# Expert activations taken in pairs on ScalarE, in the PEER stage of a two-block transformer kernel

## The reference

```python
def block(args):
    xc, ic, gc = args                       # 128 tokens, their expert numbers and gates
    u = jnp.take(expert_u, ic, axis=0)
    act = jax.nn.gelu(jnp.einsum('cd,ced->ce', xc, u).astype(jnp.float32), approximate=False)
    vv = jnp.take(expert_v, ic, axis=0)
    return jnp.einsum('ce,ced->cd', (gc * act).astype(vv.dtype), vv)
```

## Time and profile before

| | |
|---|---|
| median of 3 runs | 2718.56 us (2718.0 to 2720.35) |
| profiled execution, its own time | 2720.35 us |
| its span, first to last instruction | 2718.2 us |
| mean granted TensorE clock | 0.958 of full speed |
| busy share of the span: PE, DVE, ACT, POOL | 86%, 58%, 43%, 36% |
| bytes moved by DMA | 771 MB, of these 545 MB by GpSimd's queue |
| first and last gather issued | 657.34 and 1956.95 us |

### The profile page before, as it was taken

The page is one execution under the profiler, slowest core; times in us unless marked ns, Lnnn a source line. Parts: engine busy times, 40 slices in busy tenths (PEclk is TensorE's granted clock), DMA queues, the critical chain, the costliest instruction groups (busy, mean ns, idle before and its releaser), DMA issues. The chain is left out here.

```text
span 2718.2 us, 46334 instructions
## 1 busy us (share of the span) xinstructions
PE 2350.4 (86%) x17098; PEld 1367.4 (50%) x17098; DVE 1578.7 (58%) x3721; ACT 1156.7 (43%) x2887; POOL 990.7 (36%) x687
## 2 busy tenths in 40 slices
PE   7998799988999987777777777877889988889996
PEld 5775699956454532222222222222269777643333
DVE  6786765466566667676767667666454474420003
ACT  4535433344344454444444444444354333433343
POOL 0000211111345366676666766666601000123331
PEclk9999899989999999999999999999999957989998
DMA  8753200063999999999999999999932310389994
GB/s 312 296 198 119 83 4 4 12 253 144 393 416 409 417 411 421 421 421 421 421 419 414 415 417 411 411 421 417 381 111 79 101 32 2 150 328 371 363 365 161
DMA packets 156929, 771.24 MB, mean 284 GB/s; under 512 B 34192, under 2 KB 52256, under 8 KB 71200
## 3 DMA queue, kind: packets, MB, share of 16 engines
q0 software_dynamic: 87552, 545.34, 49.0%
q1 hardware_dynamic: 68144, 220.64, 21.5%
q10 hardware_dynamic: 1008, 2.29, 0.2%
HBM read 816.42 MB, written 16.78 MB: 307 GB/s over the span
## 5 line engine op out<-in xcount | busy, mean ns | idle before, releaser
L2239 PE MATMUL bank<-expert_rows,diagonals 128*128 128x512 f32 x1656 | 802.8, 610 | 176.9 <-ACT diagonals L2131 176.2
L2029 POOL DMA_INDIRECT expert_rows<-in_uv,expert_idx x414 | 629.7, 1521 | 464.3 <-PE bank L2239 297.4
L2064 DVE SCALAR_TENSOR_TENSOR expert_rows<-expert_rows,h_rows 128x1024 f32<-128x1024 f32 x414 | 507.4, 1226 | 328.5 <-DMA expert_rows<-in_uv,expert_idx 327.5
L2239 PEld LDWEIGHTS bank<-expert_rows,diagonals 128*128 128x128 f32 x1656 | 288.6, 189 | 636.9 <-ACT diagonals L2131 412.5
L2123 ACT ACTIVATE expert_act<-expert_dot 128x1 f32<-128x1 f32 x512 | 103.7, 203 | 692.2 <-DVE expert_rows L2064 535.1
L2239 PE MATMUL bank<-weight_slots,diagonals 128*128 128x512 f32 x392 | 193.5, 617 | 47.5 <-ACT diagonals L2131 46.9
L2131 ACT ACTIVATE diagonals<-ident,expert_weight 128x128 f32<-128x128 f32 x512 | 205.4, 401 | 16.7
L2029 POOL DMA_INDIRECT weight_slots<-in_uv,expert_idx x98 | 175.6, 1792 | 67.5 <-issue 50.7
L2064 DVE SCALAR_TENSOR_TENSOR weight_slots<-weight_slots,h_rows 128x1024 f32<-128x1024 f32 x98 | 120.1, 1225 | 88.6 <-DMA weight_slots<-in_uv,expert_idx 83.7
L2127 ACT ACTIVATE expert_weight<-expert_act,expert_gate 128x1 f32<-128x1 f32 x512 | 150.8, 295 | 17.2 <-ACT expert_act L2123 0.2
L2239 PEld LDWEIGHTS bank<-weight_slots,diagonals 128*128 128x128 f32 x392 | 66.6, 189 | 172.2 <-ACT diagonals L2131 119.1
(11 more groups left out here) (566 smaller groups left out, 4025.0 us busy)
## 6 DMA issues: line engine op xcount, KB each, us to landing
expert_w<-in_experts SPq DMA_DIRECT2D x55, 1024.0 KB, 12.1
expert_w_more<-in_experts SPq DMA_DIRECT2D x41, 1024.0 KB, 10.4
mod_rows<-in_ada_rows SPq DMA_DIRECT2D x32, 1024.0 KB, 6.7
weight_slots<-in_w_in SPq DMA_DIRECT2D x8, 1536.0 KB, 7.1
mixed<-in_ada_rows SPq DMA_DIRECT2D x10, 1024.0 KB, 5.0
weight_slots<-in_w_in SPq DMA_DIRECT2D x4, 2048.0 KB, 9.9
weight_slots<-in_att_bias SPq DMA_DIRECT2D x8, 1024.0 KB
weight_slots<-in_w_out SPq DMA_DIRECT2D x4, 2048.0 KB, 8.5
```

The costliest lines, as they stand in the source:

```text
L2029: pool.indirect_dma_start(rows[j], None, core.dram["uv"], bass.IndirectOffsetOnAxis(idx[:, t, column:column + 1], 0)).then_inc(arrived[j], 16)
L2064: dve.scalar_tensor_tensor(out=u, in0=u, scalar=1.0, in1=hN[:, t, :], op0=ALU.mult, op1=ALU.mult, accum_out=dot[:, j:j + 1]).then_inc(dott ...
L2239: mm = pe.matmul(bank[2 * (t % 2) + half][:, :], diag[:, j, :], rows[slot_of(n)][:, D + half * S:D + half * S + S], start=column == 0, sto ...
```

## The change

ScalarE takes the steps in pairs. It waits for two products, makes one gelu of two columns, then two weights, then two diagonals. Each weight still has its own gate, and each diagonal its own matmuls. VectorE's wait for a place in `expert_dot` and the columns at which work between blocks is done are written in terms of pairs. The copies of the query banks come after the pair that follows the one in which a bank was filled.

```diff
-    DEPTH, AHEAD = 8, 2
+    DEPTH, PAIR, AHEAD = 8, 2, 2
...
                     if n >= DEPTH:
-                        dve.wait_ge(gelued, n - DEPTH + 1)
+                        dve.wait_ge(gelued, (n - DEPTH) // PAIR + 1)
...
-                    if t >= 1 and column == 5:
+                    if t >= 1 and column == 3 * PAIR - 1:
                         add_block(t - 1)
-                    if t >= 1 and column == 64:
+                    if t >= 1 and column == 32 * PAIR:
                         invert_block(t - 1)
...
-                for n in range(N):
+                for pair in range(N // PAIR):
+                    n = pair * PAIR
                     (t, column), j = divmod(n, HK), n % DEPTH
                     if n % TOPK == 0:
                         act.wait_ge(topk.head_ready, 2 * (n // TOPK) + 2)
-                    act.wait_ge(dotted, n + 1)
+                    act.wait_ge(dotted, n + PAIR)
                     if n >= DEPTH:
-                        act.wait_ge(weighed, n - DEPTH + 1)
-                    act.activation(act_out[:, j:j + 1], dot[:, j:j + 1], ACT.Gelu).then_inc(gelued, 1)
-                    act.wait_ge(gelued, n + 1)
-                    if n >= DEPTH:
-                        act.wait_ge(diagonal, n - DEPTH + 1)
-                    act.activation(weight[:, j:j + 1], act_out[:, j:j + 1], ACT.Identity, scale=gates[:, t, column:column + 1]).then_inc(weighed, 1)
-                    act.wait_ge(weighed, n + 1)
-                    if n >= DEPTH:
-                        act.wait_ge(slot_free, n - DEPTH + 1)
-                    act.activation(diag[:, j, :], core.ident[:, :], ACT.Identity, scale=weight[:, j:j + 1]).then_inc(diagonal, 1)
+                        act.wait_ge(weighed, n - DEPTH + PAIR)
+                    act.activation(act_out[:, j:j + PAIR], dot[:, j:j + PAIR], ACT.Gelu).then_inc(gelued, 1)
+                    act.wait_ge(gelued, pair + 1)
+                    for i in range(PAIR):
+                        if n >= DEPTH:
+                            act.wait_ge(diagonal, n - DEPTH + i + 1)
+                        act.activation(weight[:, j + i:j + i + 1], act_out[:, j + i:j + i + 1], ACT.Identity,
+                                       scale=gates[:, t, column + i:column + i + 1]).then_inc(weighed, 1)
+                    for i in range(PAIR):
+                        act.wait_ge(weighed, n + i + 1)
+                        if n >= DEPTH:
+                            act.wait_ge(slot_free, n - DEPTH + i + 1)
+                        act.activation(diag[:, j + i, :], core.ident[:, :], ACT.Identity, scale=weight[:, j + i:j + i + 1]).then_inc(diagonal, 1)
                     for u in range(EARLY, len(units)):
-                        if ended[u] + 2 == n:
+                        if ended[u] // PAIR + 1 == pair:
                             copy_unit(u)
...
-                    if t >= 1 and column == 3:
+                    if t >= 1 and column == PAIR:
                         copy_block(t - 1)
-                    if t >= 1 and column == 17:
+                    if t >= 1 and column == 8 * PAIR:
                         square_block(t - 1)
-                    if t >= 1 and column == 49:
+                    if t >= 1 and column == 24 * PAIR:
                         root_block(t - 1)
...
-                    if t >= 1 and column == 3:
+                    if t >= 1 and column == 2 * PAIR - 1:
                         turn_block(t - 1)
-                    if t >= 1 and column == 31:
+                    if t >= 1 and column == 16 * PAIR - 1:
                         sum_block(t - 1)
```

## The result

The changed kernel takes 2738.87 us (median of 4 runs, 2736.16 to 2738.94), the kernel before took 2719.15 us in the runs beside it (4 runs, 2718.0 to 2720.35). The ratio is 1.007, with a 95% interval of 1.0052 to 1.0088: 19.7 us slower, where 7.7 were forecast. Its profiled execution took 2736.94 us with a span of 2735.1 us, 16.9 over that of before.

A forecast was written before the change was run, and what follows sets the result against it. The prediction took saturated DMA, about 2.485 us a gather, to bound the expert stage. Terms 1.8 (end) + 4.7 (6-slot pace) + 1.2 (gather 113) = 7.7 us took the median 2718.56 to 2726.3, range 2720 to 2735.

The forecast's parts named there:

- the slot that comes free later: Expert stage: issue ends 9.55 us after the slot's product, was 7.02 (8 slots) and 7.86 (6); free with 8 slots.
- The end: After the expert stage's last product: nothing covers the last pair, so its last matmul finishes 1.80 us later.
- The issue that falls into a product: Gather issue overlapping VectorE's two-input product: the lock makes it end at 9.55 us instead of 8.6.
- the sum without the lock: Expert stage: product to end of the slot's next issue, if VectorE's product did not hold up the issue: 8.6 us.
- The start: First pairs of the expert stage: later diagonals still wait behind TensorE's other work, cost nothing; uncovered 2.57 us, once.
- the rest: Query-bank copies, work between blocks and gelu table loads: delays absorbed by existing waiting, no term in the sum.
- I take 6.01: 6-slot part: assumed need from issue to product, us; pace 2.593, 0.065 a gather over 72 gathers, 4.7 us (0 to 19.8).
- rival 2: 6-slot part: short of slots in full, need 7.27 or a missed issue place; 23.6 us slower, 2742; chance 0.06.
- (9.55 + need) / 6: 6-slot part: pace per gather, from issue end after the slot's product plus need; 2.34 to 2.803 us.
- Gather 113: 6-slot part: GpSimd idles some 2 us too long before this issue, no margin absorbs it; 1.2 us (0.5 to 2).
- Rival 1: 6-slot part: need only 4.5 to 5.4 us, delay hidden; 1.8 to 3.8 us slower, 2720.4 to 2722.4; chance 0.37.
- Rival 3: Early expert stage, products 6 to 11: fewer ScalarE instructions gain 4.9 us less 1.8; 2715.5; chance 0.03.

The follow-up runs named there:

- wait_for_two: The changed kernel with two one-column gelus behind the common wait in place of one two-column gelu; 2735.56 us, ratio 1.0061 to the kernel before.
- pairs_seventh: The changed kernel with a seventh slot for steps 0 to 97; 2721.55 us, ratio 1.0009 to the kernel before.
- late_pairs: The kernel before with pairs only from step 120 on, single steps earlier; 2719.19 us, ratio 1.0003.
- early_pairs: The kernel before with pairs only for steps 0 to 119, single steps after; 2733.71 us, ratio 1.0055.
- pairs_no_lock: The changed kernel with VectorE's product replaced by a sum over u alone, reading one on-chip tensor instead of two; 2728.92 us, ratio 1.0043 to the kernel before.
- single_5_slots: The kernel before, no pairs, with 5 slots in place of 6 up to step 119 and 7 in place of 8 after; 2738.59 us, ratio 1.006.
- pairs_6_throughout: The changed kernel with 6 slots for all 512 steps; 2825.9 us, ratio 1.0397 to the kernel before.
- single_4_slots: The kernel before, no pairs, with 4 slots up to step 115 and 6 after; 2786.61 us, ratio 1.0253.
- single_6_throughout: The kernel before, no pairs, with 6 slots for all 512 steps; 2718.69 us, ratio 1.0004.

## Why the prediction was right and wrong

**Right, by the runs.** ScalarE isn't the bound and saves nothing: wait_for_two has the old number of gelus and the new time. The mechanism is the slot that comes free later: 9.50 at product 500, for 9.55 forecast, and pairs_seventh, which has the same delay and one slot more, loses nothing in the stage. It costs nothing with 8 slots (late_pairs: stage 1304.92), and with 6 slots 12.8 us (early_pairs). The end, 1.80, was measured at 1.77. The issue that falls into a product was costed at 1 us and is that, though not every issue does (mean 1.29 us in products 60 to 112, one reason why the first half of the loop is 9.12 and not 9.55); without it, in pairs_no_lock, the loop has 8.77 where the sum without the lock was 8.6. That 9.12 lies so near to 9.55 is in part luck. The forecast put the delay on top of the 5.08 us from product to issue that the 8-slot part has; between products 60 and 112 it was 6.18 before and is 7.84 now, so that of 1.80 to 2.57 us of delay only 1.66 came through, on a base 1.1 higher. The 7.86 that the forecast named as the old value with 6 slots was one row; the mean was 7.34. The start costs nothing: products 0 to 18 took 49.1 us before and 48.4 after. So does the rest: 0.5 us.

**Wrong: the step "I take 6.01" for what a gather needs from issue to product.** It gave 2.593 and 4.7 us. In its place stand, as means, 7.37 in the changed kernel, 7.25 in early_pairs and 7.26 in single_5_slots, so that this is no matter of one execution. With 9.12 before it, the pace is 2.76. Over the 72 gathers the prediction counted, against the 2.528 that the earlier trace rows bound, that would be 72 x 0.232 = 16.7 us. Measured between the same products of both kernels it was 14.4 (3.0 from 29 to 47, 11.4 from 60 to 112), three times the 4.7. The whole of products 0 to 120 lost 17.6: 1.7 more between 18 and 30 and between 47 and 60, where the forecast had nothing, 2.2 from 112 to 120, and 0.7 less at the start. The 7.37 is close to rival 2's need, 7.27, to which I gave 0.06. (The forecast's upper end is also mis-added: 1.8 + 11.3 + 2 is 15.1, not 16, and ends at 2733.7.)

**Why 6.01 was the wrong kind of number.** For a late gather it was about right: by the table of leads it takes some 6.2 on the mean. But the formula (9.55 + need) / 6 wants the mean of all gathers, those included that wait in the queue. Gathers in step come 2.48 us apart on the mean and not faster, so a gap is not won back; it only gives the next gathers in the loop more lead. By distance between products, 60 to 112 in the changed kernel: 37 at 2.7 us or less, with a mean of 2.49, and 15 above, with a mean of 3.42; before 48 and 4. In pairs_6_throughout it is 90 gaps with a mean of 3.65 among 371 (130 to 500), and many lie exactly six gathers apart. There the slow bursts carry a gap from one round to the next; between 60 and 112 the clock was 1.00, and they have no part in it. The gathers in step wait in a queue for their turn, 63% of them 7 to 8.5 us from issue to product, and the one whose issue was latest pays. So I read it: the pace is that of the worst slot of a round, not of the mean slot. It is argued, not shown. The forecast went through one even slot, and so its 2.9 us of lead, which the table prices at 0.5 to 0.9 us each time it occurs, was spread to 0.065 a gather.

What makes one slot worse than another is shown in part. In pairs_6_throughout the even gather's issue ends 9.37 after its product, the odd one's 8.61, and 71 of the 90 gaps are at even ones. The even issue falls into a product more often (in the changed kernel 1.41 us a mean issue, 1.16 for the odd). Taking that away, in pairs_no_lock, took away some 7 to 10 us. Why a gather takes 6.2 us on the mean with another one in flight, but 4.5 when it comes to an empty queue (single_4_slots, and gather 6 in the earlier trace rows), and why of two with the same 2.9 us of lead one comes in step and the other late, no run here settles.

**Gather 113.** Forecast 1.2 us. In the changed kernel GpSimd paused for 4.07 us before its issue, and its product came 5.42 behind the neighbour's, where it was 3.55: 1.9. But in early_pairs the products 112 to 120 took 20.51 us, less than the 21.38 before, so this term is inside the scatter of one execution.

**Left open.** Pairs in the early part alone cost 12.8 us of stage, the whole change 18.3, though both have the same code up to gather 120, and their medians are 5.2 us apart, of which the end explains 1.8. The rest, 3.4, I put down to the way in which gaps fall in an execution. The profiled executions allow for it: with the same code up to there, products 0 to 120 took 334.6 us in the changed kernel, 328.9 in early_pairs and 331.6 in pairs_6_throughout, and 317.0, 314.8 and 315.8 in the kernel before, late_pairs and single_6_throughout. On these means the pairs cost 15.8 us there, and the 17.6 of the account is at the high end. One profiled execution of each kernel can't show more.

**The rivals.** Rival 1, hidden, had the need at 4.5 to 5.4: refuted for 6 slots, right for 8. Rival 2's price for the 6-slot part was 19.8, and 17.6 was measured in products 0 to 120; its reason, that every gather needs 7.27, isn't so, as single_4_slots shows. Rival 3, faster: nothing in any run.

## What to carry to other kernels

Batching small instructions on an engine that idles saves nothing, and the wait for the batch delays everything that the batch releases; here it was the buffers of the bounding DMA stream. Before such a change, read for each buffer how long its next transfer's issue lies ahead of the moment the previous one lands, and take the latest issue of a round, not the mean one: in these runs the saturated stream did not win back a gap. If the batch is wanted all the same, one more buffer pays for it (pairs_seventh).

## What the runs showed of the hardware that I had not expected

- TensorE's clock can fall with the pauses that pairing makes. Between pairs in the 8-slot part TensorE idles some 1.3 us (2.2 before the last pair), then runs eight matmuls. Of the changed kernel's 185 bursts for gathers 130 to 499, 12 took some 5.4 us, all after 1.9 us of idle time or more; four others after such a pause took 3.70. In pairs_6_throughout it is 43 of 185, where late gathers follow (above). The granted clock in 1100 to 1200 us is 0.97 after and 1.00 before, and at the last pair of late_pairs, pairs_seventh and pairs_no_lock the eight matmuls took 5.40 us where 3.70 is usual. The Trainium skill tells of a matmul kernel that alternates between bursts and waits on DMA and is throttled by it (TensorE: Matmul & The Clock Gate, HAM oscillation — how this bites in real kernels). The trace agrees, for bursts of 3.70 us.
- A share of 0.97 to 0.98 for DMA can hide a stream that is 8% below its rate: 381 GB/s (pairs_6_throughout, 1100 to 1200 us) where 416 were to be had (single_6_throughout).
- A gelu of 128x2 takes 203 ns, as one of 128x1: one column more adds nothing that the trace shows.
